# One buffer ring held over a whole layer program, with two late weights loaded one stage earlier and x1 kept on chip

## The chip, the core and the metric

The kernel runs on one core of one Trainium2 chip. A core has TensorE (PE in the profile; its weight loads are PEld), VectorE (DVE), ScalarE (ACT), GpSimd (POOL) and SyncE (SP, which only issues transfers here). Each engine works through its own list of instructions in order and waits on semaphores for the others. Transfers between the memory outside (HBM) and the core's on-chip memory are carried by 16 DMA engines that all queues share. The metric is the device time of one launch in microseconds; the median of several runs is compared.

## What is computed

One layer of a trunk over 128 prompt tokens and 512 latent tokens of width 1024, cut into five blocks of 128 tokens: a projection into many parts, two token mixers (an SSD scan and an mLSTM scan, both directions), a gated merge of both that gives x1, and a channel mixer (PEER) that fetches, for each token and each of 8 heads, 16 of 16,384 experts. The reference, cut to what matters here:

```python
def trunk_layer(x, mod, on_grid, ssd_h0, mlstm_c0, mlstm_n0, mlstm_m0, lp):
    sh_a, sc_a, gt_a, sh_f, sc_f, gt_f = jnp.split(mod[:, None, :], N_MOD, axis=-1)
    h = rms_norm(x, lp['g_mix_pre']) * (1.0 + sc_a) + sh_a
    proj = h @ lp['w_in']
    ...
    mixed = (gate_ssd * y_ssd + gate_ml * y_ml) @ lp['w_out']
    x1 = x + gt_a * rms_norm(mixed, lp['g_mix_post'])
    h2 = rms_norm(x1, lp['g_ffn_pre']) * (1.0 + sc_f) + sh_f
    f = peer_ffn(h2, lp['peer_w_q'], lp['peer_keys1'], lp['peer_keys2'], lp['peer_u'], lp['peer_v'])
    x2 = x1 + gt_f * rms_norm(f, lp['g_ffn_post'])

def peer_ffn(...):   # a block of 128 tokens
    ...              # top 16 of 16 x 16 candidates of each head: expert numbers e, weights gate
    act = jax.nn.gelu(jnp.einsum('thkd,td->thk', u_tab[e], xb), approximate=False)
    return jnp.einsum('thk,thkd->td', gate * act, v_tab[e])
```

## The kernel before

Every engine's list is written out by hand; nothing reorders it. Each stage is a Python function with one block of instructions for each engine, and at its end all engines meet and its semaphores are given back. There are three stages.

**Modulate and normalise** (`modulate_and_normalise`) makes the normalised input, turned so that channels lie on partitions, and leaves it in `held`.

**Project and scan** (`project_and_scan`) streams the projection's weights in chunks of 2 MB through three buffers, `w_chunk` (`W_BUFFERS`, 48 KB of each partition). `STREAM` is their order: chunks of the projection ("big") and, in between, chunks of the modulation weights ("mod"). After the first eight the work is cut into 30 units, and `weave` puts the 32 steps of the prompt's scan between them, the same way on each engine. A "mod" unit ends in a short chain that goes through SyncE: TensorE sums a row pair, VectorE adds bias and gain (`mod_par`, loaded by SyncE, L460 and L462), SyncE stores the result (`store_row`, L465) and waits for that store before it loads `mod_par` for the next (`modulation`). The stage also makes the scans' gate scalars in small tiles (`gate_scalars`), and at the end stores the prompt's final states (out_c, out_m; L832, L833). Seven of the weight chunks (`LATE_CHUNKS`) are only applied to the prompt block here; the latent blocks' share of them comes later, as 14 "late units".

**Experts** (`experts`) does the rest: the late units (`late`, L1692 on TensorE, each two groups of eight steps of 256 columns with a weight tile of 1 MB), the backward and forward scans of the four latent blocks, the merge of every block (`merge`, steps x = 21 to 61 of a list of 64), and the PEER mixer (`body`). Its buffers are tiles of its own. The largest is `expert`, a ring of eight slots of 8 KB in each partition, 64 KB in all. GpSimd fetches one expert row for each of 128 tokens into a slot (L1506, 1 MB: 4 KB of u and 4 KB of v for a token). VectorE takes the dot product with u (L1893), ScalarE makes the coefficient and a diagonal matrix from it (L1615, L1622), TensorE multiplies the diagonal with v and adds up in `acc` (L1763), and the slot is free. In the first window some slots are multiplied by VectorE instead (L1907, L1909). There are 40 heads (5 blocks of 8) of 16 rows, 640 gathers.

Before the gathers begin, the ring serves the late units: slots 6, 7 and 5 hold the first three late weights, slot 4 their results. `late(0)` on SyncE loads the first two (`late_load`, L1407), and it stands at x = 24 of the first merge, behind that merge's loads of y_ssd, y_mlstm and three parts of the projection (L1431 to L1438). On TensorE the late units 0 to 3 stand ahead of block 0's transposes (x = 32, L1702). The merge's products (L1674) need twelve pieces of three weight matrices, 1 MB each, which SyncE loads in turn into two buffers (`piece`, L1385); a piece waits until TensorE has used the one two before.

x1 of a block is made by VectorE in `T[2]`, one of the merge's tiles (L1868). ScalarE and VectorE go on from there to h2 (L1582 to L1881). SyncE stores x1 to HBM (L1459) and, later, reloads it into the tile `x1` (`load_rest`, L1473), where the block's result is added (L1994) and from which y is stored (`store_y`, L1479). SyncE waits for that store of x1 (`x1_out`) before it loads anything over the merge's tiles for the next block (`region_free`, L1389), and VectorE waits for the reload (`x1_in`) before the block's result (`block_result`). Blocks are numbered p = 0 to 4; while the heads of block p - 1 run, the scan and merge of block p are put between them.

Of the kernel before, what the change touches and what calls it, by code (L numbers as in the profile page):

```python
# [5 lines left out]
P = 128  # L6
D = 1024
KT = D // P
BLOCKS = 5
# [12 lines left out]
ALU = mybir.AluOpType  # L22
# [10 lines left out]
G_N = 232  # L33
# [8 lines left out]
W_BUFFERS = 3  # L42
# [327 lines left out]
def project_and_scan(nc, dr, t, hT, ahead):  # L370
# [4 lines left out]
    with ExitStack() as ctx:  # L375
# [29 lines left out]
        mpar_in, row_ready, row_out = sem("mpar_in"), sem("row_ready"), sem("row_out")  # L405
        (dve_steps, dve_lists, dve_weights), (act_steps, act_exponentials), (pe_sums, pe_bank_read) = gate_scalars(
            nc, t, sb, sem, S)
# [25 lines left out]
        def _(sp):  # L433
# [12 lines left out]
            def unit(k):  # L446
# [4 lines left out]
                if units[k][1] == "mod":  # L451
                    modulation(units[k][2])

# [789 lines left out]
def experts(nc, dr, t, hT):  # L1243

    with ExitStack() as ctx:
# [3 lines left out]
        expert = sb("expert", [P, RING, 2 * D])  # L1249
# [3 lines left out]
        x1, row_f, f, sq = sb("x1", [P, D]), sb("row_f", [P, D]), sb("f", [P, D]), sb("sq", [P, D], BF16)  # L1253
# [44 lines left out]
        f_mm, acc_free, ss_ready, ms_ready, root_ready, y_ready, y_out, x1_in, row_in = (  # L1298
            sem("f_mm"), sem("acc_free"), sem("ss_ready"), sem("ms_ready"), sem("root_ready"), sem("y_ready"), sem("y_out"),
            sem("x1_in"), sem("row_in"))  # L1300
# [9 lines left out]
        out_sums, out_ms, out_root, x1_ready, x1_sums, x1_ms, x1_root, h2_ready, x1_out = (  # L1310
            sem("out_sums"), sem("out_ms"), sem("out_root"), sem("x1_ready"), sem("x1_sums"), sem("x1_ms"), sem("x1_root"),
            sem("h2_ready"), sem("x1_out"))
# [13 lines left out]
        late_in, late_mm, late_free, late_out = [sem("late_in0"), sem("late_in1")], sem("late_mm"), sem("late_free"), [sem("late_out0"), sem("late_out1")]  # L1326
# [49 lines left out]
        def _(sp):  # L1376
# [45 lines left out]
            def merge(p, x):  # L1422
# [87 lines left out]
        def _(act):  # L1510
# [25 lines left out]
            def merge(p, x):  # L1536
# [43 lines left out]
                elif x == 58:  # L1580
                    act.wait_ge(x1_ready, p + 1)
                    nc.scalar.activation(sq[:, :], T[2][:, :], ACT.Square, accum_out=mss[:, 6:7])  # L1582
# [219 lines left out]
        def _(dve):  # L1802
# [18 lines left out]
            def merge(p, x):  # L1821
# [39 lines left out]
                elif x == 57:  # L1861
# [6 lines left out]
                    nc.vector.tensor_tensor(T[2][:, :], T[2][:, :], T[1][:, :], ALU.add).then_inc(x1_ready, 1)  # L1868
# [258 lines left out]
```

## Time and profile before

| | us |
|---|---|
| median of 3 runs | 2818.5 (2817.75 to 2819.37) |
| the profiled execution | 2816.61 |
| its span in the trace | 2814.9 |
| TensorE busy | 2451.0 (87%) |
| VectorE busy | 1591.0 (57%) |
| ScalarE busy | 899.7 (32%) |
| GpSimd busy | 801.1 (28%) |

The span runs from the first to the last recorded instruction. A busy share is a mean over stages with different limits; what a stage waits for is read from the chain of waits (the work that ended last, followed back from the end), from the waits of each engine, and from windows of the time line, where the DMA engines' share and rate stand beside the engines' busy time. The three stages meet at about 45 and 570 us; the gathers are issued from 737.0 to 2782.9.

### The profile page before, as it was taken

What the parts mean: (1) busy time and instruction counts of PE and PEld (TensorE: products, weight loads), DVE (VectorE), ACT (ScalarE), POOL (GpSimd) and SP (SyncE); (2) the same over time, 40 slices, a digit from 0 to 9 for tenths busy, and PEclk for the clock granted to TensorE, in tenths of its full rate; (3) what the DMA queues carried; (4) which work ended last, traced back from release to release, by engine and by line L of the source; (5) the groups of instructions that cost most, each with busy time, mean ns of one, the idle gap of its engine ahead of it and who ended that gap; (6) DMA issues with size and microseconds to landing.
All of it is one profiled execution on the core that took longest, in us unless ns stands there. A gap on an engine that the chain in (4) does not pass through costs nothing.

```text
span 2814.9 us, 26865 instructions
## 1 busy us (share of the span) xinstructions
PE 2451.0 (87%) x8530; PEld 1364.7 (48%) x8530; DVE 1591.0 (57%) x3736; ACT 899.7 (32%) x2386; POOL 801.1 (28%) x705
## 2 busy tenths in 40 slices
PE   6999999967999778799898898997898998788886
PEld 3555554344888543455444454443554444344332
DVE  2320012211478775798655797556787557666664
ACT  3110111021123332555323554333544324343332
POOL 0111100000133122343333433334343334444452
PEclk9999999988999899999999999999999999989999
DMA  6222325856799789999999999999999999999996
GB/s 254 97 97 97 112 71 224 319 200 229 294 341 377 287 340 421 412 411 384 420 421 421 419 371 408 421 421 422 404 373 420 420 421 411 422 417 420 418 417 279
DMA packets 146016, 951.02 MB, mean 338 GB/s; under 512 B 17186, under 2 KB 28706, under 8 KB 41810
## 3 DMA queue, kind: packets, MB, share of 16 engines
q0 software_dynamic: 96928, 687.39, 59.8%
q1 hardware_dynamic: 35714, 213.68, 19.5%
q10 hardware_dynamic: 13232, 48.24, 4.4%
q8 instruction: 67, 1.10, 0.2%
q14 instruction: 75, 0.61, 0.1%
HBM read 911.44 MB, written 37.81 MB: 337 GB/s over the span
## 4 chain that ended last, share of the span: by engine, by line
PE 31%; DMA 28%; DVE 12%; ACT 3%; DVEq 2%; issue 2%; POOL 1%; ACTq 1%; SPq 0%; POOLq 0%
DMA e_expert<-in_peer_uv,e_idx 25%; PE e_acc L1763 15%; PE e_acc L1692 5%; DVE e_expert L1893 5%; PE e_qs L1778 3%; DMA e_wb<-in_w_out 2%; PE e_A L1674 2%; PE e_B L1674 2%; DVEq L1895 1%; ACT e_diag L1622 1%; POOL e_expert L1506 1%; DVE e_f L1909 1%; ACT e_coef L1615 1%; PE e_A L932 0%; DMA e_expert<-in_w_late 0%
## 5 line engine op out<-in xcount | busy, mean ns | idle before, releaser
L1763 PE MATMUL e_acc<-e_expert,e_diag 128*128 128x512 f32 x2368 | 1134.9, 627 | 225.4 <-ACT e_diag L1622 224.8
L1506 POOL DMA_INDIRECT e_expert<-in_peer_uv,e_idx x640 | 761.0, 1189 | 1461.4 <-PE e_acc L1763 1044.7
L1893 DVE CUSTOM_DVE_ANT_0 e_expert<-e_expert,e_xb 128x1024 f32<-128x1024 f32 x640 | 775.6, 1224 | 464.3 <-DMA e_expert<-in_peer_uv,e_idx 443.4
L1763 PEld LDWEIGHTS e_acc<-e_expert,e_diag 128*128 128x128 f32 x2368 | 456.0, 200 | 819.5 <-issue 487.4
L1612 ACT ACTIVATE e_act<-e_dots 128x2 f32<-128x2 f32 x320 | 65.1, 203 | 784.0 <-DVEq L1895 781.7
L523 PE MATMUL pj<-held,w_chunk 128*128 128x512 f32 x512 | 225.2, 593 | 0.0
L1622 ACT ACTIVATE e_diag<-ident,e_coef 128x128 f32<-128x128 f32 x592 | 206.1, 394 | 21.5 <-issue 0.4
L557 PE MATMUL pj<-w_chunk,held 128*128 128x512 f32 x352 | 160.7, 613 | 12.6 <-DMA w_chunk<-in_w_big 10.4
L1615 ACT ACTIVATE e_coef<-e_act,e_gate 128x1 f32<-128x1 f32 x640 | 153.8, 287 | 22.8 <-issue 0.7
L1778 PEld LDWEIGHTS e_qs<-e_h2T,e_w_head 128*128 128x128 f32 x1280 | 149.6, 194 | 10.7 <-issue 10.4
L1674 PE MATMUL e_B<-e_wb,e_m 128*128 128x512 f32 x320 | 147.0, 605 | 6.1 <-DMA e_wb<-in_w_out 6.1
L1778 PE MATMUL e_qs<-e_h2T,e_w_head 128*128 128x128 f32 x1280 | 151.1, 277 | 0.8 <-ACT e_h2T L1591 0.8
L523 PEld LDWEIGHTS pj<-held,w_chunk 128*128 128x128 f32 x512 | 95.0, 191 | 107.1 <-issue 107.1
L557 PEld LDWEIGHTS pj<-w_chunk,held 128*128 128x128 f32 x352 | 68.1, 197 | 95.2 <-issue 92.8
L1674 PEld LDWEIGHTS e_B<-e_wb,e_m 128*128 128x128 f32 x320 | 61.2, 195 | 84.2 <-issue 79.8
L1612 ACT ACT_TABLE_LOAD x76 | 97.5, 1283 | 1.8 <-issue 0.5
L1674 PE MATMUL e_A<-e_wb,e_m 128*128 128x512 f32 x160 | 77.4, 632 | 10.5 <-DMA e_wb<-in_w_out 10.0
L1692 PE MATMUL e_acc<-e_m,held 128*128 128x256 f32 x384 | 84.7, 380 | 0.0
L334 DVE COPY gt_sums<-pj 128x160 f32<-128x160 f32 x1 | 0.3, 325 | 143.2 <-PE pj L329 143.2
L1692 PEld LDWEIGHTS e_acc<-e_m,held 128*128 128x128 f32 x384 | 72.7, 191 | 9.4
L1692 PE MATMUL e_acc<-e_mg,held 128*128 128x256 f32 x320 | 70.4, 380 | 0.0
L525 PEld LDWEIGHTS pj<-held,w_chunk 128*128 128x128 f32 x512 | 62.2, 192 | 15.3 <-issue 15.3
(397 smaller groups left out, 2282.3 us busy)
## 6 DMA issues: line engine op xcount, KB each, us to landing
e_wb<-in_w_out SPq DMA_DIRECT2D x60, 1024.0 KB, 9.2
e_w_head<-in_w_q ACTq DMA_DIRECT2D x39, 1024.0 KB, 9.1
w_chunk<-in_w_big SPq DMA_DIRECT2D x18, 2048.0 KB, 9.2
w_chunk<-in_w_mod SPq DMA_DIRECT2D x8, 2048.0 KB, 12.4
e_expert<-in_peer_uv,e_idx POOLq DMA_INDIRECT x640, 13.2
wm<-in_w_mod SPq DMA_DIRECT2D x4, 2048.0 KB, 18.0
e_m<-scratch_mod_rows SPq DMA_DIRECT2D x15, 512.0 KB, 16.1
e_m<-scratch_xbcT SPq DMA_DIRECT2D x7, 1024.0 KB, 13.7
```

Source lines behind the costliest of these rows:

```text
L523: nc.tensor.matmul(pst[m][:, 0:LAT], w[:, j, k, m * P:(m + 1) * P], hT[:, k, P:TOK], start=(k == 0), stop=(k == KT - 1))
L525: last = nc.tensor.matmul(pst[m][:, LAT:TOK], w[:, j, k, m * P:(m + 1) * P], hT[:, k, 0:P], start=(k == 0), stop=(k == KT - 1))
L557: last = nc.tensor.matmul(to, hT[:, k8, b * P:(b + 1) * P], w[:, n % W_BUFFERS, k8, :], start=(k8 == 0), stop=(k8 == KT - 1))
L1506: nc.gpsimd.indirect_dma_start(expert[:, u % RING, :], None, dr["peer_uv"], bass.IndirectOffsetOnAxis(idx[:, h % 4, s:s + 1], 0)).then_inc ...
L1612: nc.scalar.activation(act_v[:, :], dots[:, m % 2, 2 * n:2 * n + 2], ACT.Gelu)
L1615: nc.scalar.mul(coef[:, n % 4, j:j + 1], act_v[:, j:j + 1], gate[:, m % 4, 2 * n + j:2 * n + j + 1])
L1622: last = nc.scalar.mul(diag[:, v % RING, :], t["ident"][:, :], coef[:, n % 4, v - u:v - u + 1])
L1674: last = nc.tensor.matmul(to, src[:, k * P:(k + 1) * P], wb[:, i % 2, k - 4 * part, :], start=(k == 0), stop=(k == KT - 1))
L1692: last = nc.tensor.matmul(late_to[u][:, 256 * b:256 * (b + 1)], hT[:, k, tokens], late_w[i][:, k, :], start=(k == 0), stop=(k == KT - 1))
L1763: mm = nc.tensor.matmul(acc[:, c * 512:(c + 1) * 512], diag[:, v % RING, :], expert[:, v % RING, D + c * 512:D + (c + 1) * 512], start=Fal ...
L1778: last = nc.tensor.matmul(qs[:, q * P:(q + 1) * P], w_head[:, k, q * P:(q + 1) * P], h2T[:, k, :], start=(k == 0), stop=(k == KT - 1))
L1893: nc.vector.tensor_tensor_reduce(expert[:, u % RING, 0:D], expert[:, u % RING, 0:D], xb[p % 2][:, :], 1.0, 0.0, ALU.mult, ALU.add, dots[:, ...
```

## The change

**One ring for the whole program.** The ring is allocated before the first stage, as `ring`. The three weight buffers of the projections are its slots 0 to 5 (two slots are one chunk of 16 KB in a partition), the gate scalars' small tiles lie in slot 6. Tiles that only the first two stages use (constants for cumulative sums, `small`, `cv`, `pick`) are given back before the experts' stage. In each partition the ring begins at byte 24,832; the tile `expert` began at byte 49,792.

**The first two late weights.** SyncE issues their loads into slots 6 and 7 at the last unit but one of the projections (k = 28 of 30), and no longer at `late(0)`. Their two semaphores live as long as the program, in a group of their own that is given back at its end.

**x1 in two buffers.** VectorE writes x1 of block p to `x1[p % 2]`, ScalarE and VectorE go on from there, the block's result is added there, and y is stored from there. The store and the reload of x1 go, and with them the semaphores `x1_out` and `x1_in` and their waits. From block 2 on VectorE waits, before it writes x1, for the store of y of the block two before.

The core of the diff:

```diff
+        slot_used = []
+
+        def in_slot(name, shape):
+            n = shape[1] if len(shape) == 2 else shape[1] * shape[2]
+            ap = t["ring"][:, 6, sum(slot_used):sum(slot_used) + n]
...
         (dve_steps, dve_lists, dve_weights), (act_steps, act_exponentials), (pe_sums, pe_bank_read) = gate_scalars(
-            nc, t, sb, sem, S)
+            nc, t, in_slot, sem, S)
...
                 if units[k][1] == "mod":
                     modulation(units[k][2])
+                if k == len(units) - 2:
+                    for i in range(2):
+                        sp.dma_start(t["ring"][:, 6 + i, :].rearrange("p (k n) -> p k n", n=256), dr["w_late"][i]).then_inc(t["late_in"][i], 16)
...
-        expert = sb("expert", [P, RING, 2 * D])
+        expert = t["ring"]
...
-        x1, row_f, f, sq = sb("x1", [P, D]), sb("row_f", [P, D]), sb("f", [P, D]), sb("sq", [P, D], BF16)
+        x1 = [sb(f"x1_{i}", [P, D]) for i in range(2)]
+        row_f, f, sq = sb("row_f", [P, D]), sb("f", [P, D]), sb("sq", [P, D], BF16)
...
             def region_free(p):
                 sp.wait_ge(h2_ready, p)
-                sp.wait_ge(x1_out, 16 * p)
...
             def late(u):
                 i = u // 2
-                if u == 0:
-                    late_load(0)
-                    late_load(1)
-                elif u == LATE_FIRST + 1:
+                if u == LATE_FIRST + 1:
...
-                elif x == 58:
-                    sp.wait_ge(x1_ready, p + 1)
-                    sp.dma_start(dr["x1"][b], T[2][:, :]).then_inc(x1_out, 16)
...
             def load_rest(p):
                 b = ORDER[p]
-                sp.wait_ge(x1_out, 16 * p + 16)
-                sp.dma_start(x1[:, :], dr["x1"][b]).then_inc(x1_in, 16)
                 if p <= 1:
                     sp.dma_start(row_f[:, :], mod_row(b, V_GATE_F)).then_inc(row_in, 16)
...
-                sp.dma_start(dr["out_y"][ORDER[p]], x1[:, :]).then_inc(y_out, 16)
+                sp.dma_start(dr["out_y"][ORDER[p]], x1[p % 2][:, :]).then_inc(y_out, 16)
...
-                    nc.vector.tensor_tensor(T[2][:, :], T[2][:, :], T[1][:, :], ALU.add).then_inc(x1_ready, 1)
+                    if p >= 2:
+                        dve.wait_ge(y_out, 16 * (p - 1))
+                    nc.vector.tensor_tensor(x1[p % 2][:, :], T[2][:, :], T[1][:, :], ALU.add).then_inc(x1_ready, 1)
...
-                dve.wait_ge(x1_in, 16 * p + 16)
                 dve.wait_ge(row_in, 32 if p else 16)
...
-                nc.vector.tensor_tensor(x1[:, :], x1[:, :], f[:, :], ALU.add).then_inc(y_ready, 1)
+                nc.vector.tensor_tensor(x1[p % 2][:, :], x1[p % 2][:, :], f[:, :], ALU.add).then_inc(y_ready, 1)
...
+        t["ring"], t["held"] = sb("ring", [P, RING, 2 * D]), sb("held", [P, HELD + 120])
+        held_sem = semaphores(nc, ctx, "held_")
+        t["late_in"] = [held_sem("late_in0"), held_sem("late_in1")]
...
-            ahead = {"w": held("w_chunk", [P, W_BUFFERS, KT, 512]), "ws": held("w_small", [P, KT, SMALL_M]), "cw": held("conv_par", [P, 4, 16]),
+            ahead = {"w": t["ring"][:, 0:2 * W_BUFFERS, :].rearrange("p (j h) (k n) -> p j (h k) n", h=2, n=512), "ws": held("w_small", [P, KT, SMALL_M]), "cw": held("conv_par", [P, 4, 16]),
```

Two places show what it does to SyncE's list; a row is a line of the kernel, the operation, what it writes and reads, its shape and how often it follows itself. The first place is the end of the projections and the start of the experts' stage (the rows L375 and L1375, after them L375 and L1387, are the change of stage). Before:

```order
L462 DMA mod_par<-in_gain_rows 2x512
L465 DMA scratch_mod_rows<-mod_par 2x512
L375 UNCONDITIONAL_BRANCH
L1375 UNCONDITIONAL_BRANCH
L1490 DMA e_w_head<-in_w_q 128x2048
L1491 DMA e_keys<-in_keysT 128x256
L1431 DMA e_m<-scratch_y_ssd 128x1024
L1432 DMA e_m<-scratch_y_mlstm 128x1024
L1433 DMA e_m<-scratch_proj 128x1024
L1437 DMA e_m<-scratch_proj 128x1024
L1438 DMA e_mg<-scratch_proj 128x2048
L1407 DMA e_expert<-in_w_late 128x2048 x2
```

After:

```order
L843 DMA out_c<-s_C 128x2056 x2
L844 DMA out_m<-s_mp 1x8
L463 DMA ring<-in_w_late 128x2048 x2
L476 DMA scratch_mod_rows<-mod_par 2x512
L471 DMA mod_par<-in_b_mod 2x512
L473 DMA mod_par<-in_gain_rows 2x512
L476 DMA scratch_mod_rows<-mod_par 2x512
L375 UNCONDITIONAL_BRANCH
L1387 UNCONDITIONAL_BRANCH
```

The two loads of in_w_late left the end of the first group of loads in the experts' stage and stand in the projections' stage now, behind the stores of the prompt's states and ahead of the last two stores of modulation rows.

The second place is from the second half of one block's merge to the first loads of the next, on SyncE; `e_x` is the x1 tile, `scratch_x` the copy of x1 in HBM. Before:

```order
L758 DMA e_m<-scratch_xbcT 128x2048
L1459 DMA scratch_x<-e_m 128x1024
L783 DMA e_m<-scratch_back_ssd 128x1024
L784 DMA e_wb<-scratch_back_c 128x2056
L789 DMA e_s_mp<-scratch_back_m 128x4
L806 DMA e_wb<-scratch_proj 128x4x256
L1433 DMA e_m<-scratch_proj 128x1024
L1437 DMA e_m<-scratch_proj 128x1024
L1438 DMA e_mg<-scratch_proj 128x2048
L1479 DMA out_y<-e_x 128x1024
L1473 DMA e_x<-scratch_x 128x1024
L1475 DMA e_row_f<-scratch_mod_rows 128x1024
```

After:

```order
L769 DMA e_m<-scratch_xbcT 128x2048
L794 DMA e_m<-scratch_back_ssd 128x1024
L795 DMA e_wb<-scratch_back_c 128x2056
L800 DMA e_s_mp<-scratch_back_m 128x4
L817 DMA e_wb<-scratch_proj 128x4x256
L1441 DMA e_m<-scratch_proj 128x1024
L1445 DMA e_m<-scratch_proj 128x1024
L1446 DMA e_mg<-scratch_proj 128x2048
L1482 DMA out_y<-e_x_0 128x1024
L1478 DMA e_row_f<-scratch_mod_rows 128x1024
```

The store of x1 behind the merge's pieces is gone, and so is the reload behind the store of y; the order of all the others is as it was.

## Rows read from the trace of the kernel before

**Rows 1.** the page's rate row: GB/s in 40 equal slices of the span

```profile
GB/s 254 97 97 97 112 71 224 319 200 229 294 341 377 287 340 421 412 411 384 420 421 421 419 371 408 421 421 422 404 373 420 420 421 411 422 417 420 418 417 279
```

**Rows 2.** the page's row of the gathers' queue: packets, MB, share

```profile
q0 software_dynamic: 96928, 687.39, 59.8%
```

**Rows 3.** chain of waits, 480 to 700: start us, us, what

```profile
573.44 12.28 DMA e_expert<-in_w_late
...
585.86 15.69 PE e_acc L1692 x64
...
608.45 6.91 PE e_qs L1692 x32
615.36 0.89 PE e_A L1702 x8
```

**Rows 4.** waits, 500 to 700: who waited for whom: us, times, longest

```profile
PE e_acc L1692 <- DMA e_expert<-in_w_late: 20.5, 1, 20.5
```

**Rows 5.** waits, 1300 to 2800

```profile
POOL e_expert L1506 <- PE e_acc L1763: 858.8, 383, 11.7
...
DVE e_expert L1893 <- DMA e_expert<-in_peer_uv,e_idx: 397.8, 288, 5.7
```

**Rows 6.** windows: stretch, its us, engines' busy us, PEclk, DMA share, GB/s

```profile
1315.00:1335.00 20.00, 19.98 (x84) 12.81 (x83) 16.31 (x32) 11.74 (x31) 6.28 (x7) 1.00 1.02 423
```

**Rows 7.** timeline of VectorE, 570 to 592: start us, us, line, operation

```profile
570.77 0.17 DVE L2023 MEMSET e_zero<- 128x128 f32 x1 [0.17 <-issue]
...
591.26 1.23 DVE L1838 SCALAR_TENSOR_TENSOR e_m<-e_m 128x1024 f32<-128x1024 f32 x1 [2.81 <-ACT e_m L1560]
```

**Rows 8.** windows around the stage's change

```profile
554.50:560.00 5.50, 5.50 (x15) 2.12 (x17) 0.00 (x0) 0.00 (x0) 0.00 (x0) 0.95 0.93 381
560.00:565.00 5.00, 4.20 (x20) 0.89 (x18) 2.04 (x3) 0.58 (x1) 0.54 (x1) 1.00 0.16 59
...
572.00:583.00 11.00, 0.00 (x0) 0.00 (x0) 0.14 (x1) 2.17 (x3) 0.00 (x0) 0.50 1.02 409
...
578.00:585.80 7.80, 0.00 (x0) 0.00 (x0) 2.45 (x2) 3.91 (x11) 0.00 (x0) 0.50 1.02 427
```

**Rows 9.** timeline of SyncE, 540 to 574: when each load or store is issued

```profile
541.91 0.35 SPq L444 DMA_DIRECT2D w_chunk<-in_w_mod  x1
544.55 0.25 SPq L465 DMA_DIRECT2D scratch_mod_rows<-mod_par  x1
553.68 0.25 SPq L460 DMA_DIRECT2D mod_par<-in_b_mod  x1
...
555.45 1.11 SPq L833 DMA_DIRECT2D out_m<-s_mp  x1
562.64 0.25 SPq L465 DMA_DIRECT2D scratch_mod_rows<-mod_par  x1
563.86 0.24 SPq L460 DMA_DIRECT2D mod_par<-in_b_mod  x1
...
570.03 0.34 SPq L1490 DMA_DIRECT2D e_w_head<-in_w_q  x1
```

**Rows 10.** DMA issues, 550 to 600: how many, KB each, us to landing

```profile
e_expert<-in_w_late SPq DMA_DIRECT2D x2, 1024.0 KB, 13.3
e_wb<-in_w_out SPq DMA_DIRECT2D x2, 1024.0 KB, 8.9
```

**Rows 11.** shares by line of the chain, 690 to 1010

```profile
by line: PE e_acc L1692 41.0%; PE e_qs L1778 6.1%; DVE e_f L1909 5.6%; DVE e_expert L1893 5.4%; PE e_acc L1763 4.5%; issue 2.4%; PE e_B L918 2.0%; PE e_A L969 1.7%; PE e_A L932 1.7%; PE e_B L900 1.7%; DVEq L1895 1.6%; PE e_A L848 1.5%; ACT 
```

**Rows 12.** tile scratch_x: line, count, duration ns, first and last start us

```profile
L1459 SPq DMA_DIRECT2D scratch_x<-e_m x5: 326/326/327, 683.5 to 2341.7; - x5
L1473 SPq DMA_DIRECT2D e_x<-scratch_x x5: 319/320/327, 686.1 to 2507.4; - x5
```

**Rows 13.** waits of SyncE, whole span

```profile
SPq L1389 <- DMA scratch_x<-e_m: 24.1, 3, 8.4
...
SPq L62 <- PEq L62: 3.0, 4, 1.4
```

More of the change, by code:

```diff
@@ L405, in project_and_scan @@
         mpar_in, row_ready, row_out = sem("mpar_in"), sem("row_ready"), sem("row_out")
+        slot_used = []
+        def in_slot(name, shape):
+            n = shape[1] if len(shape) == 2 else shape[1] * shape[2]
+            ap = t["ring"][:, 6, sum(slot_used):sum(slot_used) + n]
+            slot_used.append(n)
+            return ap if len(shape) == 2 else ap.rearrange("p (a b) -> p a b", b=shape[2])
         (dve_steps, dve_lists, dve_weights), (act_steps, act_exponentials), (pe_sums, pe_bank_read) = gate_scalars(
-            nc, t, sb, sem, S)
+            nc, t, in_slot, sem, S)
         chunks = [("prompt", 0)]
@@ L1297, in experts @@
         dots_ready, diag_ready = sem("dots_ready"), sem("diag_ready")
-        f_mm, acc_free, ss_ready, ms_ready, root_ready, y_ready, y_out, x1_in, row_in = (
+        f_mm, acc_free, ss_ready, ms_ready, root_ready, y_ready, y_out, row_in = (
             sem("f_mm"), sem("acc_free"), sem("ss_ready"), sem("ms_ready"), sem("root_ready"), sem("y_ready"), sem("y_out"),
-            sem("x1_in"), sem("row_in"))
+            sem("row_in"))
         branches_in, gates_in, shift_in, x_in, piece_in, piece_mm = (
@@ L1309, in experts @@
             sem("mix_turned"), sem("mixT_ready"))
-        out_sums, out_ms, out_root, x1_ready, x1_sums, x1_ms, x1_root, h2_ready, x1_out = (
+        out_sums, out_ms, out_root, x1_ready, x1_sums, x1_ms, x1_root, h2_ready = (
             sem("out_sums"), sem("out_ms"), sem("out_root"), sem("x1_ready"), sem("x1_sums"), sem("x1_ms"), sem("x1_root"),
-            sem("h2_ready"), sem("x1_out"))
+            sem("h2_ready"))
         (sp_scan, sp_scan_end, load_x, load_qk), pe_scan, act_scan, (dve_scan_init, dve_scan), (chunk_done, P_mixed, Ks_ready, hm_done, yoff_last, _) = scan_steps(
@@ L1581, in merge @@
                     act.wait_ge(x1_ready, p + 1)
-                    nc.scalar.activation(sq[:, :], T[2][:, :], ACT.Square, accum_out=mss[:, 6:7])
+                    nc.scalar.activation(sq[:, :], x1[p % 2][:, :], ACT.Square, accum_out=mss[:, 6:7])
                     act.drain()
@@ L2029, in programme @@
         sb = lambda n, s, d=F32: ctx.enter_context(nc.sbuf_tensor(n, s, d))
-        t = {n: sb(n, [P, P]) for n in ("ones", "triF", "triB", "ident", "nident", "maskF", "maskB")}
+        t = {n: sb(n, [P, P]) for n in ("ident", "nident", "maskF", "maskB")}
         t.update({n: sb(n, [P, P], BF16) for n in ("ident_16", "maskF_16", "maskB_16")})
@@ L2033, in programme @@
         t["rows"], t["skip"], t["gains"] = sb("rows", [P, R_N]), sb("skip", [P, HS]), sb("gains", [P, 6, KT])
-        t["small"], t["gates"] = sb("small", [P, BLOCKS, 48]), sb("gates", [P, BLOCKS, G_N])
-        t["cv"], t["pick"] = sb("cv", [P, KT, MOD_M]), sb("pick", [P, 112])
-        t["held"] = sb("held", [P, HELD + 120])
+        t["gates"] = sb("gates", [P, BLOCKS, G_N])
+        t["ring"], t["held"] = sb("ring", [P, RING, 2 * D]), sb("held", [P, HELD + 120])
+        held_sem = semaphores(nc, ctx, "held_")
+        t["late_in"] = [held_sem("late_in0"), held_sem("late_in1")]
         hT = t["held"][:, 0:KT * TOK].rearrange("p (k t) -> p k t", t=TOK)
@@ L2040, in programme @@
             sem = semaphores(nc, first, "ahead_")
-            ahead = {"w": held("w_chunk", [P, W_BUFFERS, KT, 512]), "ws": held("w_small", [P, KT, SMALL_M]), "cw": held("conv_par", [P, 4, 16]),
+            t.update({n: held(n, [P, P]) for n in ("ones", "triF", "triB")})
+            t["small"], t["cv"], t["pick"] = held("small", [P, BLOCKS, 48]), held("cv", [P, KT, MOD_M]), held("pick", [P, 112])
+            ahead = {"w": t["ring"][:, 0:2 * W_BUFFERS, :].rearrange("p (j h) (k n) -> p j (h k) n", h=2, n=512), "ws": held("w_small", [P, KT, SMALL_M]), "cw": held("conv_par", [P, 4, 16]),
                      "w_in": [sem(f"w_in{j}") for j in range(W_BUFFERS)], "par_in": sem("par_in")}
@@ L2100 @@
     "back_ssd": (CHUNKS, P, D), "back_c": (CHUNKS, P, HM * 2 * CE), "back_m": (CHUNKS, P, HM),
-    "y_ssd": (1, P, D), "y_mlstm": (1, P, D), "x1": (BLOCKS, P, D),
+    "y_ssd": (1, P, D), "y_mlstm": (1, P, D),
 }
```

4 lines of the change are left out of this document (2 added, 2 removed).

## The prediction

> **What bounds the kernel now.** I read the page first: its row of GB/s by slice shows two regimes, some 70 to 340 GB/s in the first third and then a plateau near 420 that lasts to the end [rows 1]. The gathers of the expert rows are most of that traffic: their queue's packets fill 59.8% of all DMA time [rows 2]. So I read the two regimes apart.
>
> In the first regime what counts is which engine waits. The chain of waits names one DMA in the middle of it: TensorE stands still from the end of the projections until the first late weights have landed, starts at 585.86, works through four late units, and only at 615.36 comes to the first transposes of block 0's merge [rows 3]. The waits give that standstill as 20.5 us in one piece [rows 4], and 12.28 us of it are the chain's load of w_late itself. The order of SyncE's rows shows why the weights come late: they are the eighth and ninth load of the new stage, behind some 4.3 MB of others.
>
> In the second regime GpSimd waits for ring slots (858.8 us) and VectorE for gathered rows (397.8 us) [rows 5]. That by itself could be a ring that is too short or a DMA system that is full. The windows decide it: where x1 is reloaded (1315 to 1335) the DMA engines are at 1.02 and move 423 GB/s [rows 6]. A full system means that each byte taken out gives back its time.
>
> **The first late weights, loaded early.** What is saved: TensorE has nothing to wait for at the stage's start but VectorE's short constants, whose last one ends at 570.77 + 0.17 = 570.94 [rows 7]. If the weights are there, the late units start at 570.9 in place of 585.86, which is 14.9 us. TensorE starts at the low clock either way: it had stood idle since before 570, and the windows from 572 on show 0.50 granted, the 1.2 GHz level [rows 8], so the first two units should cost the same 15.69 us.
>
> Are they there? In the new order SyncE issues the pair right behind out_m, whose issue ends at 555.45 + 1.11 = 556.6 [rows 9]. From 554.5 to 560 the engines are at 0.93, busy with the two out_c stores of 1 MB each; from 560 to 565 they stand at 0.16 [rows 8]. The pair is 2.1 MB, and at the 409 GB/s of the window 572 to 583 that is 5.1 us: it runs from about 560 to 565.1, inside the hole, 5 us before the next stage's first load at 570.03. It hides.
>
> What it costs: behind it on SyncE's queue stands the store of modulation row pair 6 (562.64), and SyncE waits for that store before it issues the loads for the last one; VectorE's last step, the last store and the stage's end hang on them. With an empty queue the store took 1.2 us (562.64 to 563.86). The same store at 544.55, issued 2.6 us after a 2 MB load, held SyncE until 553.68, 9.1 us [rows 9]. So it does wait for what is ahead of it. Here what is ahead ends at 565.1, and with the usual 1.2 us it is done at 566.3: 2.4 us late. The next small transfers find the queue empty again. The ends: 0, if a store of 4 KB slips past, and 6.0, if the pair takes the 13.3 us that it took in the crowd of the stage's start [rows 10] (556.6 + 13.3 = 569.9 against 563.86). I take 2.4, since the hole at 560 is what the trace shows for this place. The gain at the start is then 14.9 - 2.4 = **12.5 us**, with ends 8.9 and 14.9.
>
> The Trainium skill (DMA: Bandwidth & Descriptors, Queues, rings and completion order) says that the write that signals a transfer lands only after every earlier write of that DMA engine. That rule speaks against putting 2 MB ahead of this store; the 9.1 us agree with it. Were there no such order, the sum would be 2.4 us better.
>
> Is something else late instead? The transposes at 615.36 also need VectorE's step at 591.26, which ends at 592.5 [rows 7] and moves 2.4 us with the stage: 594.9. The late units end at 615.4 - 12.5 = 602.9, so they still decide, with 8 us to spare. The first two pieces of w_out are issued ahead of that step of VectorE and take 8.9 us [rows 10], so they are there by 591.3 + 8.9 + 2.4 = 602.6 at the latest, before the transposes are through; covered too. From there each piece is loaded when TensorE has used an earlier one, so that whole chain moves along; and from 690 to 1000 the chain is TensorE's and VectorE's own work, with the late units in front (41%) and no load among its larger parts [rows 11]. I see nothing that stays at its old time, so the 12.5 us should reach the gathers and the end.
>
> **x1 kept on chip.** Removed: five stores and five reloads of 512 KB, the stores from 683.5 to 2341.7, the reloads from 686.1 to 2507.4 [rows 12]. The two of block 0 fall before the gathers, where nobody waits for them: nothing. The other eight fall on the plateau. At 421 GB/s, the value that most slices show [rows 1], 0.524 MB takes 1.25 us; eight of them 10.0 us. If the gathers were bound by the ring instead, 0. I take **9.0 us**: the window at such a reload is full, but a few slices per block are not (371 to 384 in the page's row), and what is won there may run into other work.
>
> The waits that go: SyncE waited 24.1 us in three places for the x1 store before loading the next scan's states [rows 13]. Those loads come up to 8.4 us sooner; no engine waits for them in the rows, so nothing. VectorE loses a wait for the reload that was long satisfied. VectorE gains one, before x1 of blocks 2 to 4, for the store of y two blocks earlier; in the program's order that store stands four heads of 16 experts ahead. Behind the wait stand VectorE's dot products, but it should never be open. The steps on x1 keep their shapes.
>
> **The rest.** The weights in six slots and the gate scalars in the seventh are the same transfers and instructions at other addresses: nothing. Slots 6 and 7 are untouched by weights, and the gate scalars are long read when the late pair lands. One more group of semaphores is given back at the very end, with a meeting of all engines: such meetings cost SyncE 3.0 us in four [rows 13], so 0.7 us.
>
> **The sum.** 12.5 + 9.0 - 0.7 = 20.8 us. The profiled execution took 2816.6 us (its span is 2814.9), so 2795.8; the median of the runs lies 1.9 us above it: **2798 us**. Own ends: with 14.9 and 10.0 it is 2794, with 8.9 and 0 it is 2810; a few us below 2794 are possible if the reloads also cost the gathers their order.
>
> **Rivals.**
> *The x1 traffic was hidden.* The gathers' pace is the ring's: a slot is filled, dotted, multiplied and freed, and the x1 copies ran in the gaps. For it: GpSimd's 858.8 us for slots. Against: share 1.02 with 423 GB/s. Only the start is won: 2818.5 - 12.5 + 0.7 = 2807.
>
> *The start is not won.* The merge of block 0 waits for its branches or for SyncE anyway, or TensorE is held up at the new stage by something that the 20.5 us hid. Only x1 counts: 2818.5 - 9.0 + 0.7 = 2810. Against: 8 us of room above. Both failing together, 2819, is the case that the change doesn't do what it says.
>
> *The queue at the end of the projections, on the slower side.* Three small transfers follow each other there (store, loads, last store). If each takes 9.1 us as at 544.55 in place of 1.2, the stage ends 23.7 us later; with 14.9 saved and x1 worth nothing that is 2818.5 + 23.7 - 14.9 + 0.7 = 2828. It is a loss from a delay of 14.2 us on, if x1 gives nothing. Against: 2.1 MB are over once, and the second and third come behind an empty queue.
>
> *The gathers become faster.* The ring's start in each partition moves from byte 49,792, which is 128 past a multiple of 256, to 24,832, a multiple of 256. If that is what holds the plateau at 421 and it rose to the 427 of plain loads between 578 and 585.8 [rows 8], the 59.8% of DMA time in the gathers, 1683 us, would shrink by 1.4%, 24 us: 2774. Against: those loads at 427 also go to tiles that start off such a multiple. 
>
> **Chances.** The forecast 0.57; x1 hidden 0.17; start not won 0.06; neither 0.08; faster gathers 0.07; slower 0.05. The range 2789 to 2810 holds the first three. About 0.2% (5.6 us, so 2812.9 to 2824.1) is what a measurement can tell from no change: faster 0.57 + 0.17 + 0.06 + 0.07 = 0.87, same 0.08, slower 0.05.
>
> **What would show it.** Right: TensorE's first late unit between 572 and 577 with no wait for w_late; the last small store of the projections some 2 us later than 567; the first transposes near 603; x1's step in block 0 some 12 us earlier; the lead over the old trace then growing by about 1.2 us at each removed copy, to 20 at the end, with the same 421 GB/s and 5 MB fewer bytes. Wrong: a lead of 12 that stays flat (x1 hidden); a plateau above 423 (addresses); a small store that waits 6 us or more, or a new wait in front of TensorE's first late unit.

## The result, and the profile after

The changed kernel takes 2777.7 us (median of four runs, 2776.99 to 2782.65) against 2818.9 for the kernel before beside it: a ratio of 0.9853, with an interval of 0.9841 to 0.9865, or about 41 us gained. The forecast was 2798 with a range of 2789 to 2810: the direction is right, the gain is twice as large.

First the part that came as forecast. The chain of waits of the changed kernel from 480 to 700 (start us, us, what), beside [rows 3]:

```profile
571.67 0.18 DVE e_zero L2027
571.84 0.04 issue
571.89 16.90 PE e_acc L1695 x64
...
595.69 6.91 PE e_qs L1695 x32
602.60 0.89 PE e_A L1705 x8
```

No load stands there any more. TensorE starts its late units at 571.89 in place of 585.86, when VectorE's short constants are done, and comes to the first transposes at 602.60; "near 603" was the forecast. The waits of the same stretch (us, times, longest) name the constants as what it waits for, beside [rows 4]:

```profile
PE e_acc L1695 <- DVE e_zero L2027: 10.6, 1, 10.6
```

The group of the 640 gathers (duration ns min/median/max, first and last start us) carries this lead to the plateau:

```profile
L1509 POOL DMA_INDIRECT ring<-in_peer_uv,e_idx x640: 932/938/1982, 724.2 to 2743.6; - x160
```

The first gather is 12.8 us earlier than before (737.0), and the last 39.3 us earlier (2782.9). So some 26 us are won while gathers run, where the forecast had some 8 or 9. The page's row of GB/s by slice, beside [rows 1], shows a plateau that has moved:

```profile
GB/s 258 99 99 99 114 54 218 331 245 214 279 352 376 291 329 426 407 409 383 426 426 426 423 385 407 427 426 426 411 372 424 426 426 410 422 426 427 427 424 282
```

Slices that were 420 or 421 are 426 or 427. The windows of the changed kernel (stretch, its us, engines' busy us, PEclk, DMA share, GB/s) say it more sharply, and they show that the engines' share hasn't changed:

```profile
1400.00:1500.00 100.00, 88.95 (x255) 42.72 (x254) 56.22 (x135) 28.24 (x87) 32.78 (x28) 0.97 1.01 427
2200.00:2300.00 100.00, 89.35 (x248) 41.48 (x248) 61.09 (x147) 32.12 (x95) 36.77 (x30) 1.00 1.01 427
```

The kernel before has these windows too:

```profile
1400.00:1500.00 100.00, 91.74 (x260) 44.50 (x259) 52.81 (x126) 27.13 (x82) 33.52 (x30) 0.95 1.01 421
2200.00:2300.00 100.00, 91.56 (x262) 43.56 (x262) 52.02 (x124) 25.38 (x77) 32.54 (x29) 0.98 1.01 421
```

The share is 1.01 in both: the DMA engines are full either way, but the same time moves 1.4% more bytes. The prediction had named just this ("a plateau above 423 (addresses)") as the sign that it is wrong. GpSimd and VectorE still wait as in [rows 5]. The totals are smaller (waits of 1300 to 2760), but so is the stretch, 1460 us in place of 1500:

```profile
POOL ring L1509 <- PE e_acc L1766: 830.2, 392, 11.7
...
DVE ring L1898 <- DMA ring<-in_peer_uv,e_idx: 372.1, 287, 5.6
```

### The profile page after: what moved, and what is told of

The parts are those of the page before. It is cut to its first block, busy times and chain, and to the rows that moved or that the text cites. A ratio compares the mean times of both kernels' runs of the same rounds, so it can differ in the third digit from the quotient of the medians.

```text
span 2775.8 us, 26857 instructions
## 1 busy us (share of the span) xinstructions
PE 2437.5 (88%) x8530; PEld 1359.7 (49%) x8530; DVE 1590.1 (57%) x3736; ACT 899.7 (32%) x2386; POOL 800.3 (29%) x705
## 4 chain that ended last, share of the span: by engine, by line
PE 32%; DMA 26%; DVE 10%; ACT 4%; issue 2%; DVEq 2%; POOL 1%; ACTq 1%; POOLq 0%
DMA ring<-in_peer_uv,e_idx 25%; PE e_acc L1766 15%; PE e_acc L1695 5%; DVE ring L1898 4%; PE e_qs L1781 3%; PE e_B L1677 2%; DMA e_wb<-in_w_out 2%; PE e_A L1677 1%; ACT e_diag L1625 1%; POOL ring L1509 1%; DVEq L1900 1%; DVE e_f L1914 1%; ACT e_coef L1618 1%; PE e_A L943 0%; ACT e_mg L1003 0%
## 5 line engine op out<-in xcount | busy, mean ns | idle before, releaser
L1766 PE MATMUL e_acc<-ring,e_diag 128*128 128x512 f32 x2368 | 1122.8, 621 | 213.5 <-ACT e_diag L1625 213.3
L1509 POOL DMA_INDIRECT ring<-in_peer_uv,e_idx x640 | 760.3, 1188 | 1426.8 <-PE e_acc L1766 1024.3
L1898 DVE CUSTOM_DVE_ANT_0 ring<-ring,e_xb 128x1024 f32<-128x1024 f32 x640 | 775.1, 1224 | 437.5 <-DMA ring<-in_peer_uv,e_idx 416.5
L1766 PEld LDWEIGHTS e_acc<-ring,e_diag 128*128 128x128 f32 x2368 | 450.3, 197 | 800.2 <-issue 481.8
L534 PE MATMUL pj<-held,ring 128*128 128x512 f32 x512 | 225.2, 593 | 0.0
L568 PE MATMUL pj<-ring,held 128*128 128x512 f32 x352 | 158.9, 607 | 11.3 <-DMA ring<-in_w_big 9.1
L1781 PEld LDWEIGHTS e_qs<-e_h2T,e_w_head 128*128 128x128 f32 x1280 | 150.7, 195 | 10.8 <-issue 10.4
L534 PEld LDWEIGHTS pj<-held,ring 128*128 128x128 f32 x512 | 94.9, 190 | 107.3 <-issue 107.3
L568 PEld LDWEIGHTS pj<-ring,held 128*128 128x128 f32 x352 | 67.3, 195 | 93.0 <-issue 90.6
L1914 DVE SCALAR_TENSOR_TENSOR e_f<-ring,e_coef,e_f 128x1024 f32<-128x1024 f32 x47 | 60.4, 1284 | 16.6 <-ACT e_diag L1625 7.6
```

What stands on the lines that cost most here:

```text
L534: nc.tensor.matmul(pst[m][:, 0:LAT], w[:, j, k, m * P:(m + 1) * P], hT[:, k, P:TOK], start=(k == 0), stop=(k == KT - 1))
L568: last = nc.tensor.matmul(to, hT[:, k8, b * P:(b + 1) * P], w[:, n % W_BUFFERS, k8, :], start=(k8 == 0), stop=(k8 == KT - 1))
L1509: nc.gpsimd.indirect_dma_start(expert[:, u % RING, :], None, dr["peer_uv"], bass.IndirectOffsetOnAxis(idx[:, h % 4, s:s + 1], 0)).then_inc ...
L1766: mm = nc.tensor.matmul(acc[:, c * 512:(c + 1) * 512], diag[:, v % RING, :], expert[:, v % RING, D + c * 512:D + (c + 1) * 512], start=Fal ...
L1781: last = nc.tensor.matmul(qs[:, q * P:(q + 1) * P], w_head[:, k, q * P:(q + 1) * P], h2T[:, k, :], start=(k == 0), stop=(k == KT - 1))
L1898: nc.vector.tensor_tensor_reduce(expert[:, u % RING, 0:D], expert[:, u % RING, 0:D], xb[p % 2][:, :], 1.0, 0.0, ALU.mult, ALU.add, dots[:, ...
```

## The experiments

The theory after the result: the 41 us are three separate gains, some 12 from the late weights, some 10 from the x1 traffic, and some 19 because the ring now begins at a multiple of 256 bytes in each partition. The rivals for the last part: the other tiles' new addresses, a better mix of traffic without the x1 copies, or waits that are gone. The first kernel below keeps the copies and the waits, so a gain there speaks against the last two. Ratios are against the kernel before, run on the same chip.

### Only the ring's address

b_ring0 is the kernel before with a pad of 128 bytes ahead of its ring and one behind, so that the ring begins at a multiple of 256 (byte 49,920); the tiles behind it move by 256 and keep their remainder. The weight buffers of the projections, which come first behind `held` too, move with the ring. b_rest128 has the pad behind the ring alone: the tiles behind it move by 128 and get the remainders that they have in the changed kernel, the ring stays.

In both, right behind the ring:

```diff
+        sb("shift_rest", [P, 32])
```

and in b_ring0, behind `held`, which lies ahead of the ring:

```diff
+        sb("shift_ring", [P, 32])
```

> The kernel before with one change: 128 unused bytes of each partition stand ahead of the ring and 128 behind it, so that the ring starts at byte 49,920 (a multiple of 256) in place of 49,792 (128 past one) and every later tile keeps its remainder. Three theories of the 18 us that neither the early weights nor x1 account for. A, the ring's start: the plateau rises from 421 to 427 GB/s, and 1.3% of some 1500 us of plateau is 18 to 20 us: 2800 +- 4. B, the start of other tiles (weights of the heads, merge tiles): nothing, 2819, plateau 421. C, no address at all, but fewer bytes, the absent scratch tensor or the waits that went: nothing, 2819, plateau 421.

> The kernel before with 128 unused bytes of each partition behind the ring: the ring stays 128 past a multiple of 256, and the experts' other tiles get the remainders that they have in the changed kernel (weights of the heads 0, merge tiles 64). A, the ring's start: nothing, 2819, plateau 421. B, the other tiles: 2800 +- 4, plateau 427. C: nothing, 2819.

b_ring0 took 2800.0 us, a ratio of 0.9933 (0.9920 to 0.9946): 18.9 us won by the ratio, 20.4 by the medians, with nothing but addresses. b_rest128 took 2817.6, 0.9992 (0.9983 to 1.0001): nothing, so it isn't the tiles behind the ring. Nor is it the projections: the gathers of b_ring0 begin only 0.9 us earlier than before and end 16.4 us earlier.

```profile
L1507 POOL DMA_INDIRECT e_expert<-in_peer_uv,e_idx x640: 932/938/1986, 736.1 to 2766.5; - x160
```

The windows, of b_ring0 first:

```profile
1400.00:1500.00 100.00, 92.75 (x268) 44.49 (x266) 52.03 (x120) 25.65 (x78) 34.80 (x30) 0.98 1.01 426
2200.00:2300.00 100.00, 90.27 (x260) 43.65 (x259) 54.48 (x127) 27.13 (x82) 36.60 (x28) 0.97 1.01 426
```

and of b_rest128:

```profile
1400.00:1500.00 100.00, 89.20 (x263) 42.83 (x262) 52.83 (x126) 27.02 (x82) 35.22 (x30) 1.00 1.01 421
2200.00:2300.00 100.00, 91.95 (x263) 43.80 (x262) 51.62 (x127) 26.23 (x79) 31.30 (x29) 0.98 1.01 421
```

The other way round, a_ring128 is the changed kernel with its ring pushed 128 bytes past a multiple of 256; the tiles behind it move by 256.

```diff
+        sb("shift_ring", [P, 32])
         t["ring"] = sb("ring", [P, RING, 2 * D])
+        sb("shift_rest", [P, 32])
```

> The changed kernel with 128 unused bytes ahead of the ring and 128 behind it: the ring starts at 24,960, 128 past a multiple of 256, all else keeps its remainder. A, the ring's start: the plateau falls back to 421 and the time goes up by 18 to 20 us to 2796 +- 4, near what was forecast. B and C: nothing, 2778, plateau 427.

It took 2795.9, 0.9926 (0.9907 to 0.9945): 20.9 us faster than before (15.5 to 26.2 by the interval), and 18 to 21 slower than the changed kernel (18.2 by the medians, 0.0073 by the ratios). This kernel is the change as the prediction had costed it, all parts at work and the ring off a multiple; the prediction's sum was 20.8 us. That the two agree to 0.1 us is luck, since the interval is much wider. Its windows and its gathers:

```profile
1400.00:1500.00 100.00, 85.19 (x252) 40.95 (x251) 53.87 (x126) 27.03 (x82) 32.77 (x27) 1.00 1.01 422
2200.00:2300.00 100.00, 90.94 (x265) 43.64 (x264) 56.15 (x135) 28.27 (x87) 36.58 (x30) 0.99 1.01 422
```

```profile
L1509 POOL DMA_INDIRECT ring<-in_peer_uv,e_idx x640: 935/942/1991, 725.0 to 2761.1; - x160
```

The lead over the kernel before is 12.0 us at the first gather (12.8 in the changed kernel) and 21.8 at the last in place of 39.3. Nearly all of the difference arises on the plateau. The projections' weights lie in the same shifted slots, and no price of theirs shows.

### How far off, and how even

a_ring64 pads the ring 64 bytes past a multiple of 256 (16 and 48 in place of the two 32 in the diff above), and a_ring512 puts it on a multiple of 512 (64 in place of the first 32, no second pad). a_merge0 leaves the ring and pads 192 bytes ahead of the merge's tiles, so that they and the buffers of w_out begin on 256:

```diff
+        sb("shift_merge", [P, 48])
```

> The changed kernel with 64 unused bytes ahead of the ring and 192 behind: the ring starts 64 past a multiple of 256, all else keeps its remainder. If any start off the multiple costs the same (one more piece for each row of 8 KB), as with 128: 2796 +- 4, plateau 421. If the cost goes with the distance from the multiple below (half of that at 128), 2787 +- 3, plateau 424. If only 128 is bad, 2778.

> The changed kernel with the ring at byte 25,088, a multiple of 512 (and all later tiles 256 further), in place of 24,832, a multiple of 256 alone. If 256 is all that counts, 2778 +- 2 and a plateau of 427; if a coarser multiple gives more, 2770 or less.

> The changed kernel with 192 unused bytes ahead of the merge's tiles, so that these and the buffer of the w_out pieces start on a multiple of 256 too (64 past one in the changed kernel). If every tile that a transfer fills pays for its start, some 80 MB on the plateau gain 1.3%, 2 to 3 us: 2775. If only the gathers pay, 2778.

a_ring64 took 2799.1, 0.9925 (0.9912 to 0.9939), the same as 128 past:

```profile
1400.00:1500.00 100.00, 86.20 (x255) 41.26 (x253) 52.97 (x123) 26.22 (x80) 32.56 (x28) 1.00 1.01 421
```

a_ring512 took 2778.4, 0.9859 (0.9843 to 0.9876), and a_merge0 2779.4, 0.9857 (0.9842 to 0.9873): both are the changed kernel over again. So at the two offsets tried the price doesn't grow with the distance, more than 256 buys nothing, and the merge's tiles don't pay measurably. By the times alone that says little: plain loads fill them on the plateau, and the 2 to 3 us that were at stake are less than these runs can tell. The DMA packets in the next section say more.

### The gathers alone

g_ring0 and g_ring128 keep the ring and the 640 gathers, leave out the whole computation of the layer and store zeros ahead of the gathers; the two differ by 128 bytes of padding ahead of the ring. From g_ring0 to g_ring128:

```diff
-        sb("fill", [P, 32])
+        sb("fill", [P, 64])
         ring = sb("ring", [P, RING, 2 * D])
```

> Gathers alone: 640 gathers of 128 rows of 8 KB into a ring of eight slots that starts on a multiple of 256 bytes; each waits only for the landing of the one eight places before. The layer's computation is left out whole, and the outputs are filled with zeros. If the gathers keep the DMA engines full by themselves, 671 MB at 427 GB/s are 1572 us between the first and the last.  This is the pair to the next run.

> The same with the ring 128 bytes past a multiple of 256, also without the layer's computation. If the transfer itself pays for the start of its rows, 1.2 to 1.6% slower than the run before: 421 GB/s, some 20 to 25 us more. If the cost comes from engines that read and write the ring while it is filled, no difference (under 3 us), since no engine touches it here.

They took 1619.7 (1617.54 to 1622.79) and 1637.0 (1634.97 to 1639.42): 17.3 us, or 1.07%, a little under the 20 to 25 expected. The rates by slice, of g_ring0 first:

```profile
GB/s 332 427 427 428 419 412 426 427 427 427 427 428 422 417 412 427 427 427 428 427 426 414 428 427 427 427 427 428 420 423 427 427 428 427 427 427 417 410 428 294
```

```profile
GB/s 331 422 422 422 421 396 423 422 422 422 422 422 407 419 422 422 422 422 422 422 401 417 417 422 422 422 421 422 422 411 422 423 421 422 421 422 405 413 422 283
```

No engine reads or writes the ring here, and no other loads or stores run beside the gathers. The levels are those of the full kernels all the same: it is the transfer that pays for the address, not a collision with VectorE or TensorE.

The traces also hold the duration of every DMA packet; one row of a gather is a packet of 8 KB. In g_ring0 99% of them take exactly 309 ns; in g_ring128 35% do, and most others 311 to 321. In the changed kernel it is 98% (from 1300 to 2700 us), in a_ring128 44%.

Plain loads behave otherwise. Those of SyncE's queue on the plateau, also packets of 8 KB, take 309 ns in 97% of the cases in b_ring0, although the merge's tiles, which most of them fill, begin 192 bytes past a multiple there, and in 99% in a_merge0, where they begin on one: their own address shows next to nothing. With the ring 128 past they are slower too (36% in a_ring128), beside the slowed gathers. And the two early late weights, loaded into the ring before any gather, have 309 ns as their usual time in both kernels (79% of the packets in the changed kernel, 82% in a_ring128). So the ring's address is paid by its gathers and by what runs beside them, not by plain loads into it; what sets the gathers apart, no run here shows.

### The late weights and x1, one at a time

a_late_old is the changed kernel with the two first late weights loaded where they were; a_x1_spill is the changed kernel with x1 stored, reloaded and waited for as before. For a_late_old:

```diff
-                if k == len(units) - 2:
-                    for i in range(2):
-                        sp.dma_start(t["ring"][:, 6 + i, :].rearrange("p (k n) -> p k n", n=256), dr["w_late"][i]).then_inc(t["late_in"][i], 16)
...
+                if u == 0:
+                    late_load(0)
+                    late_load(1)
```

The core for a_x1_spill (x1 is `T[2]` again, with the waits on both sides):

```diff
+                elif x == 58:
+                    sp.wait_ge(x1_ready, p + 1)
+                    sp.dma_start(dr["x1"][b], T[2][:, :]).then_inc(x1_out, 16)
...
+                sp.wait_ge(x1_out, 16 * p + 16)
+                sp.dma_start(x1[:, :], dr["x1"][b]).then_inc(x1_in, 16)
```

> The changed kernel with the first two late weights loaded where they were, in the experts' stage. If the start's lead of 12.8 us at the first gather reaches the end, 2790.5 +- 3, and the first late unit starts near 585.9 again. If the start's lead is swallowed by the plateau, 2778 to 2783.

> The changed kernel with x1 stored to HBM and reloaded as before (same tiles, same places, ring still on a multiple of 256, late weights still early). If the copies are paid on the plateau, 4.2 MB at 427 GB/s: 9.8 us more than the changed kernel, 2787 +- 3, with the lead growing over the kernel's second half. If they were hidden between the gathers, 2778, and the plateau of 427 alone makes up the second half's gain.

a_late_old took 2790.2 (its four runs spread from 2781.9 to 2793.6), 0.9883 (0.9867 to 0.9898): 8 to 12 us of the gain gone, by ratios or medians. In its waits from 500 to 700 TensorE's old standstill is back, and with it the first gather at 737.1:

```profile
PE e_acc L1695 <- DMA ring<-in_w_late: 20.0, 1, 20.0
```

a_x1_spill took 2789.1, 0.9888 (0.9872 to 0.9903): 10 to 11 us gone. Its plateau stays high, so the x1 copies don't set the rate; the 10.9 us that it loses between the first and the last gather are near the time of their bytes (4.2 MB at 427 GB/s are 9.8 us). The run puts the copies and their waits back together, so that the waits have no part in it is not shown apart.

```profile
1400.00:1500.00 100.00, 88.03 (x259) 41.84 (x257) 54.57 (x127) 27.02 (x82) 34.05 (x30) 1.00 1.01 427
```

```profile
L1515 POOL DMA_INDIRECT ring<-in_peer_uv,e_idx x640: 932/938/1997, 728.9 to 2759.2; - x160
```

The three undone parts sum to 18.2 + 12.5 + 11.4 = 42.1 us by the medians, or to 0.0138 of the time by the ratios, where the whole change gave 41.2 us or 0.0147. They add up, within what the runs can tell.

### The store behind the early pair

The changed kernel's SyncE rows (start us, us, line, operation), beside [rows 9], show what the pair does to the small store behind it (L476):

```profile
554.14 2.27 SPq L463 DMA_DIRECT2D ring<-in_w_late  x2
558.60 0.25 SPq L476 DMA_DIRECT2D scratch_mod_rows<-mod_par  x1
564.80 0.25 SPq L471 DMA_DIRECT2D mod_par<-in_b_mod  x1
...
568.05 0.23 SPq L476 DMA_DIRECT2D scratch_mod_rows<-mod_par  x1
570.93 0.34 SPq L1493 DMA_DIRECT2D e_w_head<-in_w_q  x1
```

SyncE goes on 6.2 us after it has issued the store, where the forecast had 3.6 (1.2 and the 2.4). In the six kernels that issue the pair there, this ranges from 4.7 (a_merge0) to 8.3 us (a_ring512). But counted from the pair's own issue (554.14 here) it is 10.6 to 10.9 us in all six, whether the store was issued 2.3 or 6.2 us after the pair. The DMA packets show the reason: the pair's run from 558.3 to 564.7 here, and in all six SyncE goes on within 0.4 us of the last one's end. So the store ends with what is under way, and issuing it sooner doesn't help.

Two kernels tried to win this back. a_late_act issues the pair on ScalarE's queue; a_late_split keeps it on SyncE, but takes it apart: one load goes ahead of the store of modulation rows before (540.03), the other ahead of the stores of out_c (554.08). a_late_act, in ScalarE's list:

```diff
+                if k == len(units) - 2:
+                    for i in range(2):
+                        act.dma_start(t["ring"][:, 6 + i, :].rearrange("p (k n) -> p k n", n=256), dr["w_late"][i]).then_inc(t["late_in"][i], 16)
```

a_late_split, in SyncE's list; `early(i)` loads late weight i, and between the two cuts stand that unit's store and loads of modulation rows:

```diff
+                if k == len(units) - 3:
+                    early(1)
...
+                if k == len(units) - 3:
+                    early(0)
```

> The changed kernel with the early pair of late weights issued on ScalarE's queue, when TensorE has finished the last unit but one, so that it is not ahead of SyncE's store of modulation rows on the same queue. That store held SyncE 6.2 us in the changed kernel against 1.2 before. If it waited because of the order on its queue, the store takes 1 to 2 us again and the time falls by 3 to 5 us, 2774. If a transfer's signal waits for the other queues' writes on the same DMA engines, or the engines are simply full, the store is as late as before, 2778 or a little more.

> The changed kernel with the early pair of late weights split: the second goes out one unit earlier, behind the last two weight chunks, the first behind the next loads of mod_par, so that less stands ahead of the store of modulation rows that held SyncE 6.2 us. If that store is what costs the start, it takes 1 to 3 us again, the experts' stage starts 3 us sooner and the time is 2775; if the loads then delay the weight chunks instead, TensorE waits 2 to 3 us more for a chunk and the time is 2778 to 2781.

a_late_act took 2780.4, 0.9860 (0.9844 to 0.9875), and a_late_split 2780.6, 0.9866 (0.9849 to 0.9882): no gain from either. In a_late_act ScalarE issued the pair and SyncE had nothing of it ahead of its store:

```profile
559.06 1.51 ACTq L619 DMA_DIRECT2D ring<-in_w_late  x2
```

```profile
561.63 0.25 SPq L473 DMA_DIRECT2D scratch_mod_rows<-mod_par  x1
567.50 0.24 SPq L468 DMA_DIRECT2D mod_par<-in_b_mod  x1
```

It still waited 5.9 us, so SyncE's own order isn't the cause (the pair's packets go on until 568.9 there, past the store's end). In a_late_split half of the pair is gone by then, but the stores of out_c are right ahead, and it waits 8.9 us, until their packets are through (565.5):

```profile
556.58 0.25 SPq L480 DMA_DIRECT2D scratch_mod_rows<-mod_par  x1
565.43 0.24 SPq L475 DMA_DIRECT2D mod_par<-in_b_mod  x1
```

So what is under way on the DMA engines holds the store up, whoever issued it. The Trainium skill (DMA: Bandwidth & Descriptors, Queues, rings and completion order) says that a transfer's signal lands after every earlier write of that DMA engine; the 5.9 us across two queues agree with that, but engines that share their time among queues would delay the store too, and no run here tells the two apart.

## Why the prediction was wrong, point by point

**The bound of each regime: right.** TensorE's standstill at the stage's start and full DMA engines on the plateau are what the parts paid by. The rival of a ring-bound plateau falls: a_x1_spill gives 10 to 11 us back for 5.2 MB of copies, 4.2 of them on the plateau.

**The start: right, 12.5 forecast.** The first gather came 12.8 us earlier. That it is so close is partly luck: TensorE began 14.0 us earlier, and its first two units took 16.90 us in place of the same 15.69, as the granted clock stayed at its lower level (1.2 GHz) until 577.6, 5.7 us into them, against 589.2 or 3.3 us before (the other ten kernels with the layer show 15.8 to 17.0 us for these units, with and without the pair). Over the kernels of this case the six with the pair there have their first gather at 724.2 to 728.9, the four without at 736.1 to 738.2, 10.8 us apart in the mean. The delay that the sum took off was 2.4. The store was held longer than forecast (6.2 us), so one of the prediction's signs of being wrong, a small store that waits 6 us or more, did come, without costing the start. It was issued earlier too (558.60 against 562.64), and what counts is the stage's first load. With the pair ahead it stands at 570.93, and in the five other kernels that issue the pair there at 571.31 to 574.65, against 570.03 [rows 9] and, in the three others without the pair, 568.28 to 570.05. That is 0.9 to 4.6 us against [rows 9], in the mean 2.8. Neither the rival of a start not won nor the one of a slower queue came about: the last small store stands at 568.05, 0.9 us later than the 567.15 of before.

**x1 on chip: right.** 9.0 forecast, 10.0 as the upper end; undone it cost 10 to 11, and the runs can't tell these apart. The new wait of VectorE for y shows in no row.

**The meeting: small, as forecast.** SyncE's time in such meetings went from 3.0 us in four [rows 13] to 3.3 in five, 0.3 us where 0.7 was taken:

```profile
SPq L62 <- PEq L62: 3.3, 5, 1.3
```

**The rest, "the same transfers and instructions at other addresses: nothing": wrong.** This is the step that failed. For the projections' weights it held; for the ring, as the target of 640 gathers of 1 MB each, the new address was worth 18 to 21 us, nearly half of the result. The rival "the gathers become faster" had the place, the level (427) and nearly the size (24 us), and got a chance of 0.07. With the other parts it would have given 2774, 4 us from the result.

The argument against that rival was the fault: "those loads at 427 also go to tiles that start off such a multiple". That row [rows 8] is a stretch of 7.8 us with plain loads alone. It showed that off-multiple tiles can be filled at 427 by these; it didn't show that the gathers, which go on for some 2000 us, lose nothing by it. The same stretch shows why it could not decide: with the ring 128 past (b_rest128, first) and on a multiple (b_ring0, 1.75 us earlier like its stage) it moves 427 either way, although two of its loads go into the ring itself.

```profile
578.00:585.80 7.80, 0.45 (x1) 0.48 (x2) 2.45 (x2) 4.42 (x11) 0.00 (x0) 0.50 1.03 427
```

```profile
576.25:584.05 7.80, 0.52 (x1) 0.50 (x2) 2.45 (x2) 4.43 (x11) 0.00 (x0) 0.50 1.02 427
```

A row of one kind of transfer was taken as evidence on another. What could have been asked of the old trace is why the plateau, which is mostly gathers, held 421 at share 1.01 when that stretch held 427 at 1.02. The price was bounded from both sides nowhere in the sum; with an end of 24 us the range would have reached to 2774 and held the result.

## What to carry to other kernels

When a change moves a large buffer, work out the start of its old and new place in each partition, modulo 256, and price it if that buffer is the target of gathers that keep the DMA engines full; 128 bytes of padding ahead of it (and 128 behind, to keep the other tiles' remainders) were worth 0.7% here, with no other edit. A plateau at share 1.01 isn't a ceiling until its GB/s has been held against the best stretch of the same trace, and a stretch of another kind of transfer raises the question but doesn't answer it. Where gains lie in different regimes (a standstill at the start, bytes on the plateau, the rate of the plateau) they add, and each can be undone alone.

## What the runs showed of the hardware

- Gathers of rows of 8 KB into a tile that begins off a multiple of 256 bytes in its partition run at 421 or 422 GB/s in place of 426 or 427, with the DMA engines' share at 1.01 in both. 64 and 128 past cost the same, a multiple of 512 is no better than one of 256, and with nothing beside them 640 gathers take 1637.0 us in place of 1619.7. The usual packet of 8 KB takes 309 ns; off the multiple more than half take 2 to 12 ns longer.
- For plain loads no such price is seen. The late pair's packets take 309 ns in 79% of the cases with the ring on a multiple and in 82% with it 128 past (a_ring128), the projections' packets of 16 KB 611 ns at the median in both, and loads into the merge's tiles 309 ns off and on a multiple (97% in b_ring0, 99% in a_merge0). Beside gathers into a ring off the multiple plain loads are slowed too (309 ns in 36%, a_ring128).
- A small store behind the two 1 MB loads on its own queue is signalled 4.7 to 8.3 us after its issue, and 10.6 to 10.9 us after the loads' issue began, in all six kernels; with the loads on another engine's queue it takes 5.9 us, behind one of the loads and the stores of out_c 8.9. Without the pair ahead it is 1.2 to 2.9 us in four kernels.
